# The RWKV scan of a decoder kernel: TensorE's program as two loops over rounds, one lane per direction

## The chip, the cores and the metric

The kernel runs on one core of one Trainium2 chip. The metric is the time of one execution on the device, in microseconds (us). PE is TensorE (PEld its weight loads), DVE is VectorE, ACT is ScalarE, POOL is GpSimd, SP is the engine that issues most transfers.

## The reference

The program computes a small diffusion-style decoder with 256 context tokens and 256 latent tokens: a mixer layer with two gated scans, convolutional feed-forward layers, one RWKV-7 layer, sparse attention layers, and a mixture of experts. The change concerns the recurrence of the RWKV-7 layer alone. It has 16 heads of 64 and goes over the tokens in both directions; each latent scan starts from its direction's last context state.

```python
def rwkv7_scan(r, w, k, v, kk, a, S):
    # S_t = S_{t-1} (diag(w_t) - kk_t^T (a_t * kk_t)) + v_t^T k_t ;  y_t = S_t r_t
    xs = tuple(jnp.moveaxis(t.astype(jnp.float32), 2, 0) for t in (r, w, k, v, kk, a))
    def step(S, inp):
        rt, wt, kt, vt, kkt, at = inp
        sa = jnp.einsum("bhvk,bhk->bhv", S, -kkt)
        S = S * wt[:, :, None, :] + sa[..., None] * (kkt * at)[:, :, None, :] + vt[..., None] * kt[:, :, None, :]
        return S, jnp.einsum("bhvk,bhk->bhv", S, rt)
    S, ys = lax.scan(step, S, xs)
    return jnp.moveaxis(ys, 0, 2), S
```

## The kernel before

The scan works in chunks of 64 tokens: four chunks of context, then four of latents, in each direction. A unit is a direction `d` and a group `g` of 8 heads; four units (`RW_UNITS`) are in flight, and each has eight turns (`it`), so there are 32 unit turns. Heads lie on the 128 partitions in pairs (`HALF`), four such pairs to a unit, so a tile of a unit is 128 partitions by 4 x 64 columns.

Inside a turn the token-by-token recurrence is replaced by products of 64x64 matrices. POOL scales keys and gates with exponentials of the summed decay (`beta`, `kappa`, `alpha`; DVE makes `rho`), which ACT makes (`exp`). PE then makes, by name of the step: CT (the table of removals, beta by alpha), KB (kappa and beta turned, for the state's update; in a direction's first two context and first two latent turns also V, the values turned), LK (kappa by alpha), C (alpha by beta and by the state), LKV (the masked LK by the values). The inverse of the unit triangular matrix `e` is built in five levels: Y = c by the late half columns of `e`, D = `e` turned, E = d by y, which DVE puts into `e` with a mask. ACT copies Y and D out of PSUM. Level l needs the `e` of level l-1, so Y, D, E follow each other strictly within a unit. Then U = e by w (with R, the state by rho, in the latents), O (the output, two products), and S (the state's update, two products), which DVE adds to the state and POOL scales with `last`.

The order on each engine is written out by `rwkv_steps` and `rwkv_order`: the two directions of a group stand beside each other at each step, and the second head group runs half a turn (`RW_LATER`) behind the first, so that one group's steps fill the other's waits. The program is fully unrolled: each of PE's instructions of the scan stands in the instruction stream once for each time it runs. Waits are on constants: `ScanSteps` has one semaphore for each engine and unit and numbers the steps.

The helpers of PE issue these: `cross` 8 products 64x64 by 64 columns over the four quadrants of the array (`cross_both` by 128 columns, `cross_late` by 32), `own` 8 products that keep each head half in its own rows and columns, `turn` 2 transposes of 128x128. In the trace an fp32 product is two matmul records, each with a weight load; a transpose is one.

The expert stage at the end of the program (L4912, through `rounds` at L395) already has PE loops: `pe.Fori(1, n)` with the turn's number in waits and addresses.

Of the kernel before, what the change touches and what calls it, by code (L numbers as in the profile page):

```python
# [26 lines left out]
P = 128  # L27
# [119 lines left out]
class Counter:  # L147
# [7 lines left out]
    def at(self, n):  # L155
        return self.base + n
# [11 lines left out]
class Core:  # L168
# [14 lines left out]
    def counter(self, name, keep=False):  # L183


        if name not in self.counters:
            s = self.spare.pop() if self.spare and not keep else Counter(self.nc, self.ctx, name if keep else f"{name}_{self.stage_no}")
            s.keep = keep
            self.counters[name] = s
        return self.counters[name]  # L190

# [2826 lines left out]
RW_UNITS = [(d, g) for g in (0, 1) for d in (0, 1)]  # L3018


def rwkv_kinds(it):

    return it >= RW_TURNS, it % RW_TURNS < RW_TURNS // 2


def rwkv_steps(engine):

    steps, end = [], 2 * RW_TURNS
    for it in range(end):
        latent, fresh = rwkv_kinds(it)
        along = lambda *names: [(it, name) for name in names]
        later = lambda *names: [(it + 1, name) for name in names if it + 1 < end]
        values, out = ["V"] if fresh else [], ["O"] if latent else []
        tables = [[name for name in ("CT", "RB") if name == "CT" or rwkv_kinds(i)[0]] for i in (it, it + 1)]
        reads = ["RK"] if latent else []
        if engine == "pe":
            steps += ([] if it else along("CT")) + along("KB", "LK", "C", "LKV")  # L3040
            for l in RW_LEVELS:
                steps += along(f"Y{l}", f"D{l - 1}", f"E{l}")
            steps += along("U", *out) + later("CT") + along("S")
        elif engine == "act":
            steps += along("KB", *values, "C", "LKV")
            for l in RW_LEVELS:
                steps += along(f"Y{l}", f"D{l - 1}", *([f"exp{l - 3}"] if l in (3, 4) and it + 1 < end else []))
            steps += along("U")
        elif engine == "dve":
            steps += [] if it else along("last", *tables[0])  # L3050
            steps += along("LK", *reads, "W")
            for l in RW_LEVELS:
                steps += along(f"E{l}")
            steps += later("last", *(["rho"] if it + 1 >= RW_TURNS else []))
            steps += along(*out) + later(*tables[1]) + along("S")
        else:
            steps += along("beta", "alpha", "ident") + ([(it - 1, "state")] if it else [])
    return steps


RW_SLOTS = ["KB", "LK", "C", "LKV", *(f"{kind}{l}" for l in RW_LEVELS for kind in "YDE"), "U", "O", "CT", "S"]
RW_LATER = len(RW_SLOTS) // 2


def rwkv_slot(engine, it, step):

    if engine == "pool":
        at, it = {"beta": "E4", "alpha": "E4", "ident": "U", "state": "S"}[step], it if step == "state" else it - 1
    elif step in ("CT", "RB", "last", "rho"):
        at, it = "U" if step in ("last", "rho") else "CT", it - 1  # L3070
    elif step[0] == "D":
        at = f"D{int(step[1]) + 1}"
    elif step[:3] == "exp":
        at = f"E{int(step[3]) + 3}"
    else:
        at = {"V": "KB", "RK": "LK", "W": "LKV"}.get(step, step)
    return it * len(RW_SLOTS) + RW_SLOTS.index(at)


def rwkv_order(engine):  # L3080

    lanes = [(rwkv_slot(engine, it, step) + g * RW_LATER, g, i, it, step) for g in (0, 1) for i, (it, step) in enumerate(rwkv_steps(engine))]
    return [(it, step, [unit for unit in RW_UNITS if unit[1] == g]) for _, g, _, it, step in sorted(lanes)]


class ScanSteps:


    def __init__(self, core):
        self.sems, self.at_step = {}, {}  # L3090
        for u, unit in enumerate(RW_UNITS):
            for e in ("pe", "act", "dve", "pool"):
                self.sems[e, unit] = core.counter(f"rw_{e}_step{u}")
                steps = [(it, "exp" if step[:3] == "exp" else step) for it, step in rwkv_steps(e) if step[:3] != "exp" or int(step[3]) == u % 2]
                steps = ([(-1, "exp")] if e == "act" else [(-1, "S")] if e == "dve" else []) + steps
                for i, which in enumerate(steps):
                    self.at_step[e, unit, which] = i + 1
                self.at_step[e, unit, "all"] = len(steps)

    def wait(self, eng, e, unit, it, step):  # L3100

        s = self.sems[e, unit]
        eng.wait_ge(s.sem, s.at(self.at_step[e, unit, (it, step)]))

    def done(self, ins, e, unit):
        ins.then_inc(self.sems[e, unit].sem, 1)

    def settle(self):
        for (e, unit), s in self.sems.items():
            s.n += self.at_step[e, unit, "all"]  # L3110


def rwkv_scan_stage(core, st, rw):
# [7 lines left out]


# [3 lines left out]
    TURNS, ALL = RW_TURNS, 2 * RW_TURNS  # L3126
    with ExitStack() as ctx, core.engines_block() as block:
# [5 lines left out]
        free += [st.const[:, keeps + i * N * C:keeps + (i + 1) * N * C] for i in range(2 * TT // (N * C))]  # L3133
        used_up = iter(free)
# [5 lines left out]
        names = ("kappa", "c", "e", "y", "d", "lk", "rk", "rb")  # L3140
        T = {(d, g): {n: tile(f"{n}_{d}{g}") for n in names} for d, g in RW_UNITS}
        wide = {(d, g): core.sb(f"grow_{d}{g}", [P, N, C + 2], ctx=ctx)[:] for d, g in RW_UNITS}
        last = {(d, g): core.sb(f"last_{d}{g}", [P, 2, N], ctx=ctx)[:] for d, g in RW_UNITS}
        for u, unit in enumerate(RW_UNITS):
            keys, sources = (st.H[:, 2 * u + i].rearrange("p (two n t) -> p two n t", two=2, n=N) for i in (0, 1))
            turned = core.sb(f"turned_{unit[0]}{unit[1]}", [P, 2, N, C], ctx=ctx)[:]
            T[unit].update(keys=keys, alpha=keys[:, 0], rho=keys[:, 1], sources=sources, beta=sources[:, 0], state=sources[:, 1],
                           turned=turned, kappa_t=turned[:, 0], beta_t=turned[:, 1])
            T[unit].update(u=T[unit]["c"], w=T[unit]["lk"], grow=wide[unit][:, :, 1:C + 1])
        sync = ScanSteps(core)  # L3150
        chain, zeroed = core.counter("vector_chain"), core.counter("rw_zeroed")
        mine = lambda g: slice(g * N, (g + 1) * N)
        psum = {unit: core.psum[u].rearrange("p (r x) -> p r x", r=2) for u, unit in enumerate(RW_UNITS)}

        def chunk(d, it):
# [4 lines left out]
        def val_t(unit, it):  # L3160

            d, g = unit
            local, whole = chunk(d, it)
            return (rw.val_t if it >= TURNS else rw.v)[:, mine(g), local]

        def slot(unit, n, rows=slice(0, P)):

            return psum[unit][rows, :, n * 2 * C:(n + 1) * 2 * C].rearrange("p r (j t) -> p r j t", j=2)

        def wide_slot(unit, n, rows=slice(0, P)):  # L3170

            return psum[unit][rows, :, n * 4 * C:(n + 1) * 4 * C].rearrange("p r (j two t) -> p r j two t", j=2, two=2)

        def cell(unit, r, area, rows=slice(0, P)):

            return psum[unit][rows, r, area * N * C:(area + 1) * N * C].rearrange("p (n t) -> p n t", n=N)

        def by_slot(x):

            return x.rearrange("p (j r) t -> p r j t", r=2)  # L3180

# [4 lines left out]
        def packed(x, level):  # L3186

            return x[:, 0:C // 2].rearrange("p (b h) -> p b h", h=1 << (level - 1))

        def packed_slot(unit, n):  # L3190

            return slot(unit, n)[:, :, :, 0:C // 2]

        D_AT = {1: (0, 1), 2: (1, 1), 3: (0, 1), 4: (1, 1), 5: (0, 1)}
        SLOT = {"V": 2, "Y": 1, "E": 0, "U": 0, "R": 2, "O": 3, "S": 1}
        TABLE, READ, SOURCE = 0, 1, 0
        CELL_V = (0, 1)

        @block.tensor
        def _(pe):  # L3200
            def cross(out, products):
# [17 lines left out]
            def cross_late(out, level, x, y):  # L3219
                for j in (0, 1):  # L3220
                    for s in (0, 1):
                        for r in (0, 1):
                            k = 2 * j + s
                            ins = nc.tensor.matmul(packed(out[HALF[s], r, j], level), x[HALF[r], k], y(HALF[r], k), start=True, stop=True)
# [1993 lines left out]
```

## Time and profile before

| what | value |
|---|---|
| runs | 3264.14, 3270.95 and 3374.4 us, median 3270.95 |
| the profiled execution's own time | 3275.88 us |
| its span, first to last instruction | 3274.1 us |
| busy share of the span | PE 93%, PEld 76%, DVE 72%, ACT 54%, POOL 18% |
| mean granted TensorE clock | 0.959 of full speed |
| instruction packets of queue q8 over the span | 178, 2.92 MB |

A row of a timeline merges neighbours of one form: start, microseconds to the end of the last, line, tiles, sizes, count, and in brackets the idle time before it and what ended it. A busy time of PE is modelled: a matmul record has its end some 0.2 us after its start, although the next one starts long before. So the pitch, from one group's start to the next one's, tells PE's rate, and the durations don't.

### The profile page before, as it was taken

The numbers are of one execution on the slowest core, as the hardware profiler recorded it, in microseconds if no ns is written. First come the engines' busy times: TensorE is split into PE (matmuls) and PEld (weight loads), VectorE is DVE, ScalarE is ACT, GpSimd is POOL, SyncE is SP. The second block draws the span as 40 slices with busy tenths as digits, with TensorE's granted clock in tenths as the row PEclk, the third lists the DMA queues.
The fourth block names the chain that finished last, engine by engine and source line by source line (L and its number), as shares of the span: only waits on it lengthen the run. The fifth ranks groups of instructions, "written<-read, shape, count | busy, mean of one in ns | idle before, by whom it ended". The sixth has DMA issues, their size and how long they took to land. (4 is left out here: it accounts for less than half of the span.)

```text
span 3274.1 us, 64217 instructions
## 1 busy us (share of the span) xinstructions
PE 3035.5 (93%) x25576; PEld 2480.9 (76%) x25576; DVE 2352.6 (72%) x3467; ACT 1769.2 (54%) x2875; POOL 573.8 (18%) x620
## 2 busy tenths in 40 slices
PE   5998889999797898879999999997999999999998
PEld 4775568878673777769987888856788888888887
DVE  5868754468847334577857777654899999999998
ACT  2524343232314554345436443764788888888887
POOL 0007124321101233138323111430000000000000
PEclk8998999999898999989989998998999999999999
DMA  6535224446211000158732887402999999999997
GB/s 227 170 104 19 103 90 149 142 150 204 97 58 26 4 5 4 36 187 275 272 107 78 295 311 292 124 27 79 334 371 367 373 367 367 370 363 374 368 359 262
DMA packets 337363, 647.53 MB, mean 198 GB/s; under 512 B 23853, under 2 KB 144281, under 8 KB 337113
## 3 DMA queue, kind: packets, MB, share of 16 engines
q1 hardware_dynamic: 316233, 568.38, 51.1%
q0 software_dynamic: 20160, 73.41, 6.2%
q8 instruction: 178, 2.92, 0.4%
q10 hardware_dynamic: 720, 2.23, 0.2%
q14 instruction: 72, 0.59, 0.1%
HBM read 641.34 MB, written 1.05 MB: 196 GB/s over the span
## 5 line engine op out<-in xcount | busy, mean ns | idle before, releaser
L5011 DVE TENSOR_TENSOR weights_lo<-raw_ring,weights_hi 128x1024 fp32r<-128x1024 f32 x336 | 400.9, 1220 | 36.8 <-ACT weights_hi L4941 29.4
L4941 ACT ACTIVATE weights_hi<-raw_ring 128x1024 fp32r<-128x1024 f32 x336 | 356.8, 1065 | 91.0 <-PE bank_pair L4877 54.7
L4877 PE MATMUL bank_pair<-weights_hi,expert_x_hi 128*128 128x512 f32 x896 | 282.4, 396 | 4.9 <-DVE weights_lo L5011 4.8
L5011 DVE TENSOR_TENSOR weights_lo<-H,weights_hi 128x1024 fp32r<-128x1024 f32 x224 | 268.7, 1221 | 24.7 <-ACT weights_hi L4941 17.4
L4877 PE MATMUL bank_pair<-weights_hi,expert_x_lo 128*128 128x512 f32 x896 | 277.7, 391 | 0.0
L4877 PE MATMUL bank_pair<-weights_lo,expert_x_hi 128*128 128x512 f32 x896 | 277.3, 391 | 0.0
L4941 ACT ACTIVATE weights_hi<-H 128x1024 fp32r<-128x1024 f32 x224 | 236.5, 1060 | 58.1 <-PE bank_pair L4877 43.2
L2707 DVE SCALAR_TENSOR_TENSOR conv<-bank_pair,vec,conv 128x189 f32<-128x189 f32 (+3 forms) x396 | 138.5, 428 | 147.1 <-ACT conv L2667 147.1
L4877 PEld LDWEIGHTS bank_pair<-weights_hi,expert_x_lo 128*128 128x128 f32 x896 | 168.9, 188 | 36.2
L4877 PEld LDWEIGHTS bank_pair<-weights_lo,expert_x_hi 128*128 128x128 f32 x896 | 168.7, 188 | 36.2
L4877 PEld LDWEIGHTS bank_pair<-weights_hi,expert_x_hi 128*128 128x128 f32 x896 | 164.1, 189 | 36.4 <-issue 5.1
L1341 PE MATMUL bank_pair<-Y_parts,const_parts 128*128 128x256 f32 (+1 forms) x592 | 145.8, 331 | 1.6 <-DVE H_parts L1386 1.6
L4889 PE MATMUL bank_pair<-weights_hi,hidden_hi 128*128 128x512 f32 x448 | 138.7, 391 | 0.0
L4889 PE MATMUL bank_pair<-weights_hi,hidden_lo 128*128 128x512 f32 x448 | 138.1, 389 | 0.0
L4889 PE MATMUL bank_pair<-weights_lo,hidden_hi 128*128 128x512 f32 x448 | 138.0, 389 | 0.0
L5011 DVE TENSOR_TENSOR weights_lo<-const,weights_hi 128x1024 fp32r<-128x1024 f32 x112 | 134.0, 1219 | 3.9 <-ACT weights_hi L4941 0.5
L4941 ACT ACTIVATE weights_hi<-const 128x1024 fp32r<-128x1024 f32 x112 | 119.4, 1066 | 32.0 <-PE bank_pair L4877 21.7
L621 DVE SCALAR_TENSOR_TENSOR mod_sums_ada<-mod_ring_ada,act,mod_sums_ada 128x1024 f32<-128x1024 f32 x84 | 116.5, 1391 | 6.2 <-DMA mod_ring_ada<-in_w_ada 6.2
L1341 PEld LDWEIGHTS bank_pair<-Y_parts,const_parts 128*128 128x128 f32 x592 | 101.9, 191 | 14.0 <-DVE const_parts L1321 2.4
L1130 PE MATMUL bank_pair<-const 128*128 128x512 f32 (+1 forms) x140 | 74.9, 647 | 32.8 <-PEq L206 32.8
L1341 PE MATMUL bank_pair<-H_parts,const_parts 128*128 128x256 f32 (+1 forms) x296 | 97.8, 330 | 0.0
L4889 PEld LDWEIGHTS bank_pair<-weights_lo,hidden_hi 128*128 128x128 f32 x448 | 84.1, 188 | 17.6
(805 smaller groups left out, 8128.5 us busy)
## 6 DMA issues: line engine op xcount, KB each, us to landing
raw_ring<-in_moe_w_gate SPq DMA_DIRECT2D x64, 1024.0 KB, 6.3
raw_ring<-in_moe_w_up SPq DMA_DIRECT2D x56, 1024.0 KB, 7.0
ring_up<-in_ffn_w_up SPq DMA_DIRECT2D x110, 512.0 KB, 4.1
H<-in_moe_w_down SPq DMA_DIRECT2D x48, 1024.0 KB, 5.2
raw_ring<-in_moe_w_down SPq DMA_DIRECT2D x48, 1024.0 KB, 5.2
mod_ring_ada<-in_w_ada POOLq DMA_DIRECT2D x84, 512.0 KB, 6.4
ring_down<-in_ffn_w_down SPq DMA_DIRECT2D x66, 512.0 KB, 5.9
H<-in_moe_w_gate SPq DMA_DIRECT2D x32, 1024.0 KB, 7.2
```

The lines of the kernel that those rows point to most:

```text
L621: ins = self.core.nc.vector.scalar_tensor_tensor(total, tile, scale, total, ALU.mult, ALU.add)
L1130: core.nc.tensor.matmul(core.bank(bank)[:, cols], st.C("ones"), st.const[:, cols], start=True, stop=True)
L1341: ins = self.core.nc.tensor.matmul(self.bank(it, o)[:, 0:T], w, y, start=s == self.begin[o] and k == 0 and a == 0, stop=s == self.end[o] a ...
L2707: ins = nc.vector.scalar_tensor_tensor(out, shifted, tap(w, 2 * it + o), out, ALU.mult, ALU.add)
L4877: ins = nc.tensor.matmul(bank, x[:, k * SEATS:(k + 1) * SEATS].bitcast(F32R), w[:, j * WIDE:(j + 1) * WIDE], start=k == 0 and i == 0, stop ...
L4889: ins = nc.tensor.matmul(DOWN[half], x, w[:, half * 512:(half + 1) * 512], start=c == 0 and i == 0, stop=c == FEC - 1 and i == 2)
L4941: nc.scalar.activation(hi[:, u % CUTS].bitcast(F32R), raw_part(u), ACT.Copy).then_inc(cut.sem, 1)
L5011: nc.vector.tensor_tensor(lo[:, u % CUTS].bitcast(F32R), raw_part(u), hi[:, u % CUTS], ALU.subtract).then_inc(parted.sem, 1)
```

## The change

PE's program becomes: round -1 (preparation), `pe.Fori` over rounds 0 to 7 (context), `pe.Fori` over rounds 8 to 14 (latents), and rounds 15 and 16 unrolled. A round is one turn of one head group, `m % 2`, in each of two lanes, the directions. So every tile has one address per lane, whatever the round. What this takes:

- Tiles hold the group of the round. States live in `store0` and `store1`; POOL copies the round's into `state`, and the values into `vn`. All V are turned by PE each round.
- Waits of PE are on the loop's register. So each step of ACT, DVE and POOL has a semaphore of its own per lane, counted by rounds (`ScanSignals`, with `LAG` for steps that belong to the round before), SP sets them to a common level at the start (`align`), and each wait in a loop is followed by a `sem_inc` on PE.
- U, O and S of a round are issued in the next one (`U'`, `S'`, `O'`); CT, C (now CC) and LK in the round before (`fore`).
- In the context D is made by products with the identity (`turn_by_product`) in place of transposes; in the latents by transposes.
- RK and RB are made together after `rho` is there (RKB); one ACT copy takes the turned kappa, beta and values (768 columns), one takes U and R; one DVE copy takes both halves of CC. DVE copies `e1`, the identity with level 1, into `e` in each round. POOL adds R to the output, DVE adds O.
- `rho` moves from DVE to POOL.

```diff
-RW_UNITS = [(d, g) for g in (0, 1) for d in (0, 1)]
+RW_ROUNDS = 4 * RW_TURNS
+RW_READS = 2 * RW_TURNS
+LANES = (0, 1)
...
+def rwkv_order(engine, n):
+    late, read, more = n >= 1, n >= RW_READS, n + 1 < RW_ROUNDS
+    inside = 0 <= n < RW_ROUNDS
...
+    fore = [lane(d, "CT+", "CC+", "LK+") if more else [] for d in LANES]
+    reads, behind, kept = ["RKB"] * read, ["O'"] if n > RW_READS else [], ["S'"] if more else []
+    if engine == "pe":
+        if n < 0:
+            return fore[0] + fore[1]
+        if read:
+            behind = ["O'"]
+        if not inside:
+            return both("U'", *behind)
+        return [*both("Y2", "D1", *["R"] * read, "U'"), *both("E2", *kept, *behind), *both("Y3", "D2"), *both("V", "KB"), *both("E3", "LKV"), *both("Y4", "D3", *reads), *both("E4"),
+                *both("Y5", "D4"), *both("E5"), *lane(0, "Y6", "D5"), *fore[0], *lane(1, "Y6", "D5"), *fore[1], *both("E6")]
+    if engine == "act":
+        scales = both("shrink+", "grow+") if more else []
...
+        return [*both("Y2", "D1", *behind), *scales, *both("Y3", "D2"), *both("KB"), *both("Y4", "D3"), *both("Y5", "D4"), *both("Y6", "D5")]
+    if engine == "dve":
...
+        return [*both("copy"), *both("E2", *kept, *behind), *both("E3", "LKV"), *both(*reads), *both("E4"), *both("E5"), *fore[0], *fore[1], *both("E6"), *last]
...
+    ahead = [*both("ident+"), *both("alpha+"), *(both("scale'") if late and more else []), *both("state+", "vn+"), *both("beta+", "kappa+")] if more else []
+    return [*ahead, *(both("rho+") if more and n + 1 >= RW_READS else []), *both(*["R"] * (read and inside))]
...
+            def turn_by_product(out, x):
+                return cross(out, [(x, ident)])
+
+            def rounds_from(n, at):
+                def wait(e, lane, step):
+                    pe.wait_ge(sig.sems[e, lane, step].sem, at)
+                    if not isinstance(at, int):
+                        pe.sem_inc(carried.sem, 1)
+                        carried.n += times
...
+                    elif kind == "Y":
+                        if l == 2:
+                            wait("dve", d, "E6")
+                            wait("dve", d, "CC")
+                        else:
+                            wait("dve", d, f"E{l - 1}")
+                        e = t["e1" if l == 2 else "e"]
+                        ins = cross_late(Y[d], l, lambda rows, k: t["c"][rows, k], lambda rows, k: half_columns(e[rows, k], l, 1 - d))
+                    elif kind == "D":
+                        ins = (turn if n >= RW_READS else turn_by_product)(TURN[d], t["e1" if l == 1 else "e"])
...
+            for first, end in ((0, RW_READS), (RW_READS, RW_ROUNDS - 1)):
+                times = end - first
+                with pe.Fori(at(first), at(end)) as i:
+                    rounds_from(first, i)
+            rounds_from(RW_ROUNDS - 1, at(RW_ROUNDS - 1))
+            rounds_from(RW_ROUNDS, at(RW_ROUNDS))
```

## Rows read from the trace of the kernel before

**Rows 1.** A line's own view: durations min/median/max in ns, first to last start.
```profile
L3435 DVE TENSOR_TENSOR H<-H,bank_pair x32: 420/421/423, 1092.9 to 1372.0; 128x256 f32<-128x256 f32 x32
```

**Rows 2.** Windows: the scan, and five turns of the expert loop.
```profile
1058.00:1373.00 315.00, 282.62 (x10049) 245.93 (x10050) 126.78 (x398) 158.15 (x520) 93.06 (x152) 0.98 0.02 4
...
2600.00:3198.00 598.00, 597.89 (x2741) 495.61 (x2740) 560.38 (x519) 485.00 (x506) 0.00 (x0) 1.00 1.01 367
```

**Rows 3.** Timeline of PE in the context part of the scan.
```profile
1090.59 0.67 PE L3224 MATMUL bank_pair<-y,d 64*64 64x32 f32 x32 [0.16 <-ACT d L3351]
1091.08 0.67 PE L3207 MATMUL bank_pair<-H 64*64 64x64 f32 x32
1091.57 0.62 PE L3224 MATMUL bank_pair<-e,c 64*64 64x32 f32 x32
...
1150.10 1.10 PE L3216 MATMUL bank_pair<-H 64*64 64x128 f32 x32
1151.14 0.66 PE L3236 MATMUL bank_pair<-const 128*128 128x128 f32 x4
1151.72 0.33 PE L3230 MATMUL bank_pair<-rw_v,lk 64*64 64x64 f32 x4
...
1154.98 0.65 PE L3224 MATMUL bank_pair<-const 64*64 64x32 f32 x32
1155.57 0.66 PE L3236 MATMUL bank_pair<-const,e 128*128 128x128 f32 x4
...
1158.83 0.67 PE L3230 MATMUL bank_pair<-const 64*64 64x64 f32 x16
1159.32 0.53 PE L3230 MATMUL bank_pair<-lk,const 64*64 64x64 f32 x12
1160.42 0.33 PE L3230 MATMUL bank_pair<-lk,const 64*64 64x64 f32 x4 [0.57 <-issue]
```

**Rows 4.** Timeline of PE in the latent part.
```profile
1259.42 0.38 PE L3236 MATMUL bank_pair<-const,kappa 128*128 128x128 f32 x2
...
1259.95 0.66 PE L3265 MATMUL bank_pair<-const,rw_v 128*64 128x128 f32 x8
1260.54 0.33 PE L3236 MATMUL bank_pair<-const,kappa 128*128 128x128 f32 x1
```

**Rows 5.** Waits in the scan: us in total, times, longest.
```profile
PEld bank_pair L3236 <- issue: 7.2, 27, 1.1
```

**Rows 6.** DMA queues, in the scan and from 2600 us on: packets, MB, share.
```profile
q8 instruction: 79, 1.29, 1.7%
...
q14 instruction: 2, 0.02, 0.0%
```

**Rows 7.** Lines' own views: the expert loop's branches, the scan's separate waits.
```profile
L399 PEldq COMPARE_BRANCH  x7: 76/208/238, 2539.6 to 3257.4; - x7
...
L3103 PEldq EVENT_SEMAPHORE  x56: 51/51/51, 1090.9 to 1345.1; - x56
```

**Rows 8.** Groups of instructions in the scan: busy us, mean ns, idle before.
```profile
L3416 DVE COPY_PREDICATED e<-const,bank_pair 128x128 f32<-128x128 uint32 x80 | 22.6, 332 | 48.0 <-PE bank_pair L3224 47.8
L3344 ACT ACTIVATE y<-bank_pair 128x128 f32<-128x128 f32 x80 | 21.1, 278 | 34.4 <-PE bank_pair L3224 34.4
L3340 ACT ACTIVATE turned<-bank_pair 128x512 f32<-128x512 f32 x32 | 18.3, 596 | 17.5 <-PE bank_pair L3265 16.2 <-PE bank_pair L3236 1.3
L3369 POOL TENSOR_TENSOR kappa<-rw_k,kappa 128x256 f32<-128x256 f32 x16 | 11.7, 730 | 1.3
L3426 DVE TENSOR_TENSOR lk<-bank_pair,const 128x256 f32<-128x256 f32 x24 | 9.8, 422 | 2.7 <-PE bank_pair L3216 1.3 <-PE bank_pair L3207 0.9
...
L3421 DVE COPY_PREDICATED e<-const,bank_pair 128x256 f32<-128x256 uint32 x16 | 7.0, 463 | 0.6 <-PE bank_pair L3207 0.4
L3353 ACT ACTIVATE c<-bank_pair 128x256 f32<-128x256 f32 x16 | 6.2, 384 | 7.7 <-PE bank_pair L3230 7.4
L3404 DVE COPY last<-grow 128x4 f32<-128x4 f32 x30 | 3.4, 159 | 0.0
```

More of the change, by code:

```diff
@@ L3017 @@
 RW_TURNS = CTX // RW_CHUNK
-RW_UNITS = [(d, g) for g in (0, 1) for d in (0, 1)]
[L3021 to L3058, printed above, removed]
@@ L3061 @@
[L3061 to L3077, printed above, removed]
@@ L3080, in rwkv_order @@
[L3080 to L3086, printed above, removed]
-    def __init__(self, core):
[L3090 to L3106, printed above, removed]
+RW_ROUNDS = 4 * RW_TURNS
@@ new lines, with value, first, align @@
+class ScanSignals:
+    LAG = {"U": 1, "S": 1, "O": 1, "E6": 1, "kappa": -1}
+    STEPS = {"act": ("D1", "D2", "D3", "D4", "D5", "U", "KB", "grow", "shrink"),
+             "dve": ("CC", "LK", "E2", "E3", "E4", "E5", "E6", "S", "O", "LKV", "RKB", "last", "copy"),
+             "pool": ("alpha", "kappa", "rho", "scale", "R")}
+    def __init__(self, core):
+        self.sems = {(e, lane, s): core.counter(f"rw_{e}_{s}_{lane}") for e, steps in self.STEPS.items() for lane in LANES for s in steps}
+        self.level = max(c.base for c in self.sems.values()) + 1
+        self.pe = [core.counter(f"rw_pe_steps_{lane}") for lane in LANES]
+        self.pe_at, self.pe_n = {}, 0
+        for n in range(-1, RW_ROUNDS + 1):
+            for d, step, m in rwkv_order("pe", n):
+                if d == 0:
+                    self.pe_n += 1
+                    self.pe_at[step, m] = self.pe_n
+    def value(self, step, m):
+        return self.level + m + 1 + self.LAG.get(step, 0)
+    def first(self, step):
+        return RW_READS if step in ("R", "RKB", "rho", "O") else -1 if step in ("U", "S") else 0
+    def align(self, eng):
+        for (e, lane, s), c in self.sems.items():
+            by = self.value(s, self.first(s) - 1) - c.base
+            if by:
+                eng.sem_inc(c.sem, by)
+    def wait_pe(self, eng, lane, step, m):
+        eng.wait_ge(self.pe[lane].sem, self.pe[lane].at(self.pe_at[step, m]))
+    def wait(self, eng, e, lane, step, m):
+        eng.wait_ge(self.sems[e, lane, step].sem, self.value(step, m))
+    def done(self, ins, e, lane, step, m):
+        if (e, lane, step) not in self.sems:
+            return
+        c = self.sems[e, lane, step]
+        ins.then_inc(c.sem, 1)
+        c.n = self.value(step, m) - c.base
@@ L3108, in settle @@
     def settle(self):
-        for (e, unit), s in self.sems.items():
-            s.n += self.at_step[e, unit, "all"]
+        for c in self.pe:
+            c.n += self.pe_n
 def rwkv_scan_stage(core, st, rw):
@@ L3139, in tile @@
             return t.rearrange("p (n t) -> p n t", n=N)
[L3140 to L3155, printed above, removed]
+        names = ("shrink", "kappa", "alpha", "rho", "e1", "e", "y", "d", "lk", "w", "vn", "store0", "store1")
+        T = [{n: tile(f"{n}_{d}") for n in names} for d in LANES]
+        wide = [core.sb(f"grow_{d}", [P, N, C + 2], ctx=ctx)[:] for d in LANES]
@@ L3157, in chunk, with mine @@
+        sig = ScanSignals(core)
+        cleared, zeroed, emptied, stores, carried = (core.counter("rw_" + n) for n in ("cleared", "zeroed", "emptied", "stores", "pe_waited"))
+        front, levels = ([core.psum[2 * d + i].rearrange("p (r x) -> p r x", r=2) for d in LANES] for i in (0, 1))
+        def mine(m):
+            return slice(m % 2 * N, (m % 2 + 1) * N)
+        def chunk(d, m):
+            it = m // 2
             c = it % TURNS if d == 0 else TURNS - 1 - it % TURNS
             return slice(c * C, (c + 1) * C), slice((it >= TURNS) * CTX + c * C, (it >= TURNS) * CTX + (c + 1) * C)
[L3160 to L3176, printed above, removed]
+        def slot(pair, n):
+            return pair[:, :, n * 2 * C:(n + 1) * 2 * C].rearrange("p r (j t) -> p r j t", j=2)
@@ L3384, in _ @@
         @block.vector
         def _(dve):
-            c = Chain(dve, chain)
-            for unit in RW_UNITS:
+            for d in LANES:
                 for edge in (0, C + 1):
-                    ins = nc.vector.memset(wide[unit][:, :, edge:edge + 1], 1.0)
+                    ins = nc.vector.memset(wide[d][:, :, edge:edge + 1], 1.0)
             zeroed.count(ins)
-            for unit in RW_UNITS:
-                sync.done(nc.vector.memset(T[unit]["state"], 0.0), "dve", unit)
-            c.ended(nc.vector.memset(rw.y, 0.0))
@@ L3394, in _ @@
-            for it, step, units in rwkv_order("dve"):
-                for unit in units:
-                    d, g = unit
-                    t = T[unit]
-                    kind = step.rstrip("123456")
+            for d in LANES:
+                for name in ("e", "w", "ur", "turned"):
+                    ins = nc.vector.memset(T[d][name], 0.0)
+            cleared.count(ins)
+            for d in LANES:
+                nc.vector.memset(T[d]["rkb"], 0.0)
+            emptied.count(nc.vector.memset(rw.y, 0.0))
@@ L3436, in _ @@
-                    sync.done(ins, "dve", unit)
-        sync.settle()
+                        ins = nc.vector.tensor_copy(last[d][:, m % 2].unsqueeze(2), t["grow"][:, :, edge:edge + 1])
+                        sig.done(ins, "dve", d, step, m)
+                        continue
+                    if step == "copy":
+                        sig.wait_pe(dve, d, "U", m - 1)
+                        sig.wait(dve, "dve", d, "CC", m)
+                    elif step == "S":
+                        sig.wait_pe(dve, d, "O" if m + 1 >= RW_READS else "S", m)
+                    else:
+                        sig.wait_pe(dve, d, {"CT": "LK", "CC": "LK"}.get(step, step), m)
```

410 lines of the change are left out of this document (238 added, 172 removed).

## The prediction

> **What bounds the kernel now.** The page's busy slices and the windows view come first. TensorE (PE) is the busiest engine of the whole span, but the diff touches one stage alone, the RWKV scan. It starts on PE at 1058 us (the edge of the window in [rows 2]), and DVE's last addition to a state ends at 1372.4 [rows 1]: 314 us, 9.6% of the 3274.1 us span. In that stretch PE is busy 282.6 us (90%), ACT 50%, DVE 40%, POOL 30%, and DMA moves 4 GB/s [rows 2]. So nothing but the scan's order of work can move the time, and PE is the nearest bound.
>
> Next comes what PE's time consists of. The timeline of PE gives the pitch of a block, start to start, where nothing waits. I call a block the 16 matmul records that one helper makes for one unit (8 matmuls, each in two passes; a transpose is one record).
> - Y or E, 32 columns: two blocks in 1091.08-1090.59 = 0.49 us, 0.245 each. CT by `cross`, 64 columns: 1091.57-1091.08, the same 0.245; the columns don't count here [rows 3].
> - `cross_both`, 128 columns: 1.04 for two, 0.52 each. `own`: 1159.32-1158.83 = 0.49 each [rows 3].
> - Four transposes: 1259.95-1259.42 = 0.53 with nothing switched, so 0.26 a pair; 1151.72-1151.14 = 0.58 with the way back to 64x64. Y before a transpose takes 1155.57-1154.98 = 0.59 instead of 0.49. Going from 64x64 to 128x128 and back costs about 0.1 us each way [rows 3, 4].
> - The V turn by eight products with the identity: 0.59 [rows 4].
>
> **Work of PE before.** A unit's turn in the context: CT 0.25, KB 0.53, V 0.3 (half the turns), LK 0.25, C 0.52, LKV 0.49, ten Y/E 2.45, five D 1.55 with the switches shared by two units, U 0.49, S 0.49 = 7.3 us. In the latents CT and LK are wide (+0.54), R and O come on (+0.98): 8.8. Sixteen of each: 258 us of 314. The other 56 us are stalls; PE's busy time hides a part of them, since a record's modelled end reaches 0.2 us past the next one's start.
>
> What these waits are, by the view of waits: but for the first wait of the stage the largest kind of idle PE and of idle weight loads is "issue", a wait for nothing that the profile shows [rows 5]. The timeline shows it inside blocks that are underway: 0.57 us at 1160.42, twelve records into an `own` block that had begun at 1159.32 [rows 3]. Data can't be missing there. The instruction queue q8 brought 79 packets and 1.29 MB in the stretch, 16 KB per packet, against 20,099 matmuls and loads [rows 2, 6]: 64 bytes each, 256 a packet, one each 4.0 us. I take the stalls to fall on the borders of the fetched pieces. The loads' waits by issue are 0.27 us on the mean before transposes (7.2/27) [rows 5]; 79 x 0.28 = 22 us, with 0 and 79 x 0.57 = 45 us as the ends. The rest, some 34 us, is waits for ACT and DVE.
>
> **The change, part by part.** Lanes: before, four units are in flight; after, two (one per direction), each alternating its head groups over 16 rounds. The same 32 unit turns are done.
>
> (1) PE work after. A context round per lane: Y/E 2.45; D as eight products, 5 x 0.245 = 1.23, without a switch; U and S 0.98; V and KB three pairs of transposes, 0.83 with their switches; LKV 0.49; CT, CC, LK 1.02 = 7.0. Latents: D stays a transpose but is now one lane's at a time (`both("Y3", "D2")` is lane by lane), so 0.26 + 0.16 = 0.42 x 5 = 2.1; R, O and RKB add 1.47 = 9.3. Two lanes: 14.0 and 18.7 us a round, 8 of each: 261 us. Against 258 it is +3 us. The new D saves 0.3 per turn in the context and loses 0.55 in the latents. PE's work as such brings nothing.
>
> (2) Fetching. Two loop bodies, about 1,470 and 1,510 instructions (716 and 736 matmul records, as many loads, 34 and 40 waits), the unrolled rounds -1, 15 and 16 about 1,900: 19 pieces instead of 79. 60 borders x 0.28 = -17 us, if a body stays in place. For that speaks the expert loop: 598 us of it hold 5,481 matmuls and loads in five turns [rows 2], about 1,100 a turn, and in the 670 us from 2600 on q8 has no packet, only q14 two small ones [rows 6]. The new bodies are a third larger than that one. The Trainium skill, "Runtime: NRT & Kernel Launch", section "Instruction fetch mechanics", says both: PE holds 2,048 instructions, and a taken branch whose target is outside the current window forces a fetch before execution goes on. By its capacity the bodies stay; by its branch rule they don't, which is rival B. The trace of the expert loop agrees with the first, at the smaller size.
>
> (3) Turning back. A turn of PE's loop in the trace costs an ALU_OP, a FUSED_REGOPS of some 0.04 and a COMPARE_BRANCH of 0.208 [rows 7], about 0.3 us; there it was hidden by queued 0.39 us matmuls, here nothing is queued. 8 + 7 turns: +4 us (bounds 1 and 15, the last if the first block waits 1 us for its instructions).
>
> (4) The waits. Each wait in the loops is a register's and is followed by a `sem_inc`. The trace has 56 EVENT_SEMAPHORE on PE at 51 ns in the scan [rows 7]; 37 a round x 16 x 0.051 = 30 us if all were on the path, 0 if all are hidden. Most are satisfied early and overlap queued matmuls; 6 or 7 a round really wait. +6 us.
>
> (5) What the shorter cover costs. This is the largest term, stepped from the durations in [rows 8] (ACT 0.28 for Y and for a D of the same size, DVE E 0.33 and a little more, 0.42 for 256 columns and 0.16 for 4, so 0.68 for 512; ACT 0.38 for 256, 0.60 for 512, so 0.81 for 768), plus 0.25 from a PE block's last start to a reader's start. Context round, Y2 of lane 0 at 0: PE has Y2, D1, U' of both lanes done by 2.0, E2 and S' by 3.5, Y3 and D2 by 4.5, V and KB by 6.0, E3 and LKV by 7.8, all with ACT and DVE in time but for 0.3 us. Levels 4 and 5 have no filler: Y and D of both lanes 1.0, then E waits for ACT, the next Y for DVE's E: Y4 to Y6 of lane 0 takes 5.0 (4.8 by ACT's denser pitch) where PE has 3.5 of work. The end of the round is worse. DVE does CT, CC, LK of both lanes before E6: 2 x (0.46 + 0.68 + 0.42) = 3.1 us, at best 2.7, starting when PE has LK of lane 0. PE has issued E6 of lane 1 some 1.75 us after that start, DVE ends E6 of lane 0 2.7 + 0.36 = 3.1 us after it, and the next round's Y2 waits for that: 1.4 us of idle PE each round. Sum 17.1 us against 14.0 of work. Latents, the same way: RKB fills level 4 on PE but puts 1.4 us ahead of E4 on DVE (0.9 stall), level 5 stalls 0.4, the end 1.4: 21.4 against 18.7. POOL has kappa' ready about 1.6 us before CT needs it and is no wait yet (14 operations of up to 0.73, 8.4 to 10 us of a context round).
>
> The sum: first Y2 at about 1062.4 (PE waits for POOL, which now has stores, identities, alpha, state and value copies ahead of beta and kappa, and for DVE's `CT`, `CC`, `LK`), 8 x 17.1 + 8 x 21.4 = 308, less 3.4 in round 15, which prepares nothing, plus 3.5 for the closing U and O: 1370.5, that is 2 us earlier than now [rows 1]. On it come waits +6, turns back +4, and the 19 cold borders, 19 x 0.28 = +5. **Scan +13 us.** The profiled execution took 3275.9 us (span 3274.1), 5 us over the median of the runs. 3275.9 + 13 = 3289, as a median 3284.
>
> **The rivals.**
> - A: the filler works better than stepped. Then PE's work is what counts: 261 + 4 at the start + 10 for waits, turns and cold borders + 10 to 20 of waits, 285 to 295 against 314: -25 us, 3246. For it: ACT and DVE are at 50% and 40% now. Against: E6 stands behind both lanes' CT, CC, LK in DVE's own order, which no slack elsewhere removes. Its floor, 261 + 4, is -49 us: 2% (65 us) is out of reach while PE does this work.
> - B: the body doesn't stay in place and each turn fetches again. Then the 5 to 6 borders return, 15 x 5.5 x 0.28 = 23 us, and each jump waits for its first piece (a packet takes 1.7% x 16 x 315 / 79 = 1.1 us [rows 6]), 15 to 20 us: 3284 + 40 = 3324. Decides from the body's size somewhere above 1,100 instructions.
> - C: slower by over 2%. Two lanes are too few: each of the five levels is Y, D on PE (0.49) + 0.25 + ACT 0.50 + 0.05 + E 0.25 + 0.25 + DVE 0.36 + 0.05 = 2.2 us, and what stands between on the in-order engines delays the chain; if POOL's kappa' comes 2 us late too (POOL's operations 0.1 longer beside DVE, and started only when `grow` is through ACT's queue behind U'), a round takes 21 and 25.5, the scan 376: +62, 3333 and up. It decides when a round's chain is over 20 us; by my steps it is 17 to 21.
> - D: the loops change nothing, the fetch stalls being something else. Then -17 in (2) falls away and the rest stays: 3301.
>
> **How the numbers follow.** Forecast within its own terms (3265 to 3305) 0.42; A 0.24; D 0.10; B 0.16; C 0.08. Range 3236 to 3326: below are the best parts of A, above C and the worst of B. A measurement of this kernel tells 2% from no change. Faster by over 2% asks for more than PE's floor allows, 0.03; slower by over 2% is C and a corner of B, 0.09; within 0.88.
>
> **What the profile after would show.** Rounds of 17 and 21 us; PE work of 14 and 18.7 in them. Instruction packets in the scan: about 19, none after each loop's first turn. Idle PE by "issue" under 15 us. The largest wait of PE: Y2 for DVE's E6, about 1.4 us in each of 15 rounds. EVENT_SEMAPHORE on PE about 600 times. The other stages unchanged within a few us. I am wrong if PE's waits per round are under 1 us (A), if packets keep coming at 4 GB/s (B), or if CT waits for POOL (C).

## The result, and the profile after

| | median, us | lowest to highest | runs |
|---|---|---|---|
| before | 3271.75 | 3264.14 to 3374.4 | 18 |
| after | 3287.8 | 3277.26 to 3292.22 | 18 |

The run of 3374.4 us is a slow one, 3% above the others, and the ratio leaves it out. The ratio is 1.0045, with a 95% interval of 1.0034 to 1.0055; the medians differ by 16 us, after being the slower. The forecast was 3284. The profiled execution has a span of 3285.9 us, 11.8 more than before. The scan, from the end of DVE's drain ahead of it to DVE's last operation in it, goes from 1055.9 to 1394.9 in the trace of after and from 1052.6 to 1372.4 in that of before: 339.0 against 319.9, 19.1 us longer. All the rest together is 7.3 us shorter (3.4 longer ahead of the scan, 10.7 shorter behind it); over the traces of this study the rest varies by 14 us (2940.3 to 2954.2), though all edits of the experiments lie in the scan. So the scan alone is explained below.

The page of after: busy time, share of the span and instructions, and the instruction queue over the span. Before had 178 such packets.

```profile
PE 3040.2 (93%) x27176; PEld 2492.1 (76%) x27176; DVE 2371.4 (72%) x3483; ACT 1743.1 (53%) x2797; POOL 615.4 (19%) x720
...
q8 instruction: 117, 1.92, 0.2%
```

The queues of the scan alone, 1050 to 1400 us of after (79 packets before [rows 6]):

```profile
q8 instruction: 18, 0.29, 0.4%
```

The lines of the loops and of the separate semaphore counts, durations min/median/max in ns, first and last start:

```profile
L3350 PEldq COMPARE_BRANCH  x15: 76/208/235, 1086.3 to 1371.4; - x15
...
L3280 PEldq EVENT_SEMAPHORE  x552: 51/51/51, 1065.1 to 1371.0; - x184
```

The branches mark the turns. The windows view, cut at them: length, busy us (and instructions) of PE, its loads, DVE, ACT and POOL, granted clock, DMA share and GB/s. In order: the first context turn, the fifth, the first latent turn, and two steady latent turns.

```profile
1064.90:1086.20 21.30, 16.78 (x728) 15.28 (x725) 8.68 (x25) 8.03 (x28) 6.13 (x12) 0.98 0.01 4
...
1137.40:1154.50 17.10, 14.96 (x732) 14.05 (x727) 8.15 (x24) 8.05 (x28) 7.20 (x14) 1.00 0.00 0
1205.70:1235.30 29.60, 24.30 (x750) 21.06 (x744) 9.39 (x27) 8.71 (x28) 9.94 (x18) 0.79 0.01 3
1280.10:1301.80 21.70, 19.19 (x751) 16.81 (x746) 10.04 (x28) 8.67 (x28) 9.89 (x18) 1.00 0.00 1
1301.80:1326.40 24.60, 22.10 (x750) 19.31 (x743) 10.05 (x28) 8.71 (x28) 9.90 (x18) 0.86 0.00 0
```

Context turns 2 to 8 take 17.0 to 17.2 us, all at a granted clock of 1.00. The latent turns 2 to 7 take 23.1, 21.7, 21.7, 24.6, 21.7 and 23.1; the longer ones are those with a clock under 1.00. The first turn of each loop is the one that fetches, 5 packets in the context and 6 in the latents; the fourth context turn has one more, the others none.

PE's waits by what ended them, in the scan: us in total, times, longest.

```profile
PE bank_pair L3258 <- DVE const L3489: 27.6, 23, 1.5
PE bank_pair L3241 <- POOL const L3419: 10.9, 1, 10.9
PE bank_pair L3241 <- issue: 4.7, 4, 1.5
PE bank_pair L3258 <- ACT const L3391: 3.2, 16, 0.2
PE bank_pair L3258 <- issue: 2.3, 3, 1.6
```

L3258 is `cross_late` (Y and E), L3489 DVE's E. PE's timeline has these waits in each steady turn (start, length, idle time before it): Y2 in a context turn, then in a latent turn Y2, Y5 and the second lane's E5, which waits for ACT's copy of D4.

```profile
1139.33 0.43 PE L3258 MATMUL bank_pair<-const,cw 64*64 64x32 f32 x16 [1.49 <-DVE const L3489]
...
1282.02 0.43 PE L3258 MATMUL bank_pair<-const,cw 64*64 64x32 f32 x16 [1.50 <-DVE const L3489]
1295.82 0.43 PE L3258 MATMUL bank_pair<-const,cw 64*64 64x32 f32 x16 [0.74 <-DVE const L3489]
1297.99 0.43 PE L3258 MATMUL bank_pair<-Y,H 64*64 64x32 f32 x16 [0.26 <-ACT H L3391]
```

The first wait stands at the head of each of 15 rounds, 1.5 us in most and never under 1.1, 21.8 of the 27.6 us; Y5 in the eight latent rounds gives the rest. The wait by "issue" is 7.0 us in 7 pieces. In before the same view has four such rows:

```profile
PE bank_pair L3207 <- issue: 4.4, 6, 1.3
PE bank_pair L3230 <- issue: 3.4, 7, 0.7
PE bank_pair L3236 <- issue: 2.3, 4, 1.0
PE bank_pair L3224 <- issue: 2.2, 6, 0.8
```

That is 12.3 us in 23 pieces. Against before, then, 61 fewer packets took only 5 us out of PE's own idle time. Its waits for DVE, added over all rows of the view, went the other way: from 9.6 to 27.9 us. With those for ACT and POOL the idle time is 14.7 us longer, most of the scan's 19.1.

### The profile page after: what moved, and what is told of

Its sections match the earlier page's. It is cut to its first block and busy times, and to the rows that moved or that the text cites. A ratio compares the mean times of both kernels' runs of the same rounds, so it can differ in the third digit from the quotient of the medians.

```text
span 3285.9 us, 68297 instructions
## 1 busy us (share of the span) xinstructions
PE 3040.2 (93%) x27176; PEld 2492.1 (76%) x27176; DVE 2371.4 (72%) x3483; ACT 1743.1 (53%) x2797; POOL 615.4 (19%) x720
## 5 line engine op out<-in xcount | busy, mean ns | idle before, releaser
L3384 ACT ACTIVATE const<-bank_pair 128x128 f32<-128x128 f32 x80 | 22.5, 282 | 150.3 <-PE bank_pair L3269 80.7
```

The costliest lines, as they stand in the source:

```text
L3384: nc.scalar.activation(by_slot(t["y"])[:, :, :, 0:C // 2], Y[d], ACT.Copy)
```

## Experiments

Each ratio is to before on the same chip. The changed kernel itself, run again with the first group (`e0_after`): 3285.14 us, 1.0056 (1.0041 to 1.0071), steady turns of 17.1 and 21.7 us, scan 1.2 us shorter than in the first trace. Its latent turns at a lower clock stand elsewhere (23.2 and 23.1, at turns 3 and 5), so as far as two traces tell their places are chance. One falls in the context here, in its second turn:

```profile
1085.30:1103.90 18.60, 16.57 (x736) 15.65 (x731) 8.13 (x25) 8.24 (x28) 7.20 (x14) 0.91 0.00 0
```

> The changed kernel as it is, as the yardstick on this chip. Both theories: about 1.0045 of the kernel before, 3280 to 3292 us; context rounds 17.1 us, latent rounds 21.7 us where the clock is full. If the half-clock stretches inside the scan (five of 3.4 us and one of 10.2 us in the first profile) are a matter of chance, their places will differ here; if the stalls at fixed places bring them, they will be at the same rounds.

**The same order without loops.** PE's loops are written out: no register in a wait, no `sem_inc`.

```diff
-            for first, end in ((0, RW_READS), (RW_READS, RW_ROUNDS - 1)):
-                times = end - first
-                with pe.Fori(at(first), at(end)) as i:
-                    rounds_from(first, i)
+            for n in range(RW_ROUNDS - 1):
+                rounds_from(n, at(n))
```

> PE's rounds 0 to 14 stand in the stream one after the other, with constant waits and no sem_inc; all else as in the changed kernel. Theory S (small borders, the prediction's: 0.28 us each): about 60 pieces come back, +17 us, the separate waits (-6) and the turns back (-4) go: +7 us against the changed kernel. Rival F (a border costs what the cold first context round shows, 21.3 - 17.1 = 4.2 us for 6 pieces, 0.7 each): 7 x 4.2 in the context and as much or more in the latents, +60 us and more less 10: +50 us. Rival N (the fetch stalls are nothing): -10 us. q8 packets in the scan 80 in all cases.

3308.8 us, 1.0138 (1.0122 to 1.0154). The instruction queue has 91 packets in the scan (80 were expected). A context turn takes 19.8 to 21.4 us instead of 17.1, with 5 or 6 packets each; PE's waits by "issue":

```profile
PE bank_pair L3258 <- issue: 14.8, 15, 1.9
PE bank_pair L3241 <- issue: 14.8, 18, 1.2
...
PE bank_pair L3269 <- issue: 1.3, 1, 1.3
PE bank_pair L3250 <- issue: 1.2, 1, 1.2
```

32.1 us in 35 pieces, 25 more than with the loops; the medians differ by 24, where the three theories had 7, 50 and -10. The gain of the loops lies mostly in the context: from one KB copy of ACT to the next, latent rounds at full clock take 21.5 to 23.0 us unrolled, on the mean only 0.6 over the 21.7 with the loop. So the loops do work, and the loss is elsewhere: the new order unrolled is 42 us over before, and the loops give 24 of it back. But what they remove is in part of the new order's own making: before had 12.3 us of such idle time with 79 packets, the new order unrolled has 32.1 with 91.

**Without loops, but with the separate counts.** As above, and each wait of rounds 0 to 14 keeps its `sem_inc`.

```diff
-                    if not isinstance(at, int):
+                    if 0 <= n < RW_ROUNDS - 1:
                         pe.sem_inc(carried.sem, 1)
```

> As the unrolled one, but each wait of rounds 0 to 14 is followed by a sem_inc on PE, as in the loops. The difference to the unrolled one is the price of the separate waits alone. Theory S: +6 us (0.05 us at the 6 or 7 waits of a round that really wait). Rival H (hidden): within 2 us. Rival G (each of the 550 costs its 51 ns): +28 us.

3381.62 us, 1.0339 (1.0319 to 1.0358): 1.0339 / 1.0138 is 2%, so 552 counts add 66 us to the unrolled kernel, 0.12 us each, with two more packets. All three theories (6, under 2, 28) were too low. Rounds take 22.4 to 31.3 us. This isn't the price of a count by itself: PE's idle time by "issue" doubles, from 32.1 to 64.1 us in 54 pieces (its two largest rows first), and the clock falls far more often:

```profile
PE bank_pair L3241 <- issue: 33.5, 26, 2.3
...
PE bank_pair L3258 <- issue: 22.9, 21, 2.2
```

```profile
1058.00:1485.00 427.00, 330.72 (x11532) 294.89 (x11528) 144.08 (x410) 134.30 (x446) 130.08 (x240) 0.86 0.02 4
```

**Twice the counts in the loops.**

```diff
-                        pe.sem_inc(carried.sem, 1)
-                        carried.n += times
+                        for _ in (0, 1):
+                            pe.sem_inc(carried.sem, 1)
+                            carried.n += times
```

> The changed kernel with two sem_inc behind each wait in the loops in place of one. The unrolled pair differed by 66 to 80 us for one sem_inc at each of 550 waits. Theory X (in the loops, where nothing is fetched, a sem_inc hides unless the wait really waits): 51 ns at 7 waits, +0.3 us a round at most, +0 to +6 us. Rival G (a sem_inc costs 0.12 us anywhere): 37 x 0.12 = 4.4 us a round, +66 us; then the loops lose as much as they gain.

3327.81 us, 1.0188 (1.0175 to 1.0202), by the ratios 1.3% or 43 us over the changed kernel, between the 0 to 6 and the 66 of the two theories. The scan has 18 packets, as before the edit, so this is no fetching. A context turn at full clock:

```profile
1190.90:1209.90 19.00, 15.77 (x735) 14.61 (x729) 8.31 (x25) 8.05 (x28) 7.22 (x14) 1.00 0.00 0
```

1.9 us for 34 more counts, 0.056 each. A latent round without lowered clock, from one KB copy of ACT to the next, takes 22.8 against 21.7: 1.1 for 40. On top, most turns have a stretch at the lower clock (20.4 and 24.3). So in the context 0.056 us of each count comes through, no less than the 0.051 that it lasts, and in the latents about half of it: most counts are on the path, and not only those where PE really waits.

**E6 ahead of the second lane's CT, CC, LK.** The part that changes of the order on PE, then of that on DVE:

```diff
- *both("E5"), *lane(0, "Y6", "D5"), *fore[0], *lane(1, "Y6", "D5"), *fore[1], *both("E6")]
+ *both("E5"), *both("Y6", "D5"), *fore[0], *both("E6"), *fore[1]]
...
- *both("E5"), *fore[0], *fore[1], *both("E6"), *last]
+ *both("E5"), *fore[0], *both("E6"), *fore[1], *last]
```

> PE and DVE do E6 of both lanes before CT, CC, LK of lane 1 (lane 0's stay ahead of E6). Theory Q (the 1.5 us at Y2 is DVE's queue in front of E6): Y2 finds E6 done; the wait moves to lane 1's CC, which comes 1 us of PE work later; a round gets 1.0 to 1.5 us shorter, -15 to -22 us. Rival P (the chain of POOL or ACT is next behind it): the 1.5 us appear at another wait and the time stays within 3 us.

3265.31 us, 1.0000 (0.9985 to 1.0015), 20 us under the changed kernel. Y2's wait, and the windows of a context and a latent turn:

```profile
1134.68 0.43 PE L3258 MATMUL bank_pair<-const,cw 64*64 64x32 f32 x16 [0.51 <-DVE const L3489]
```

```profile
1133.60:1149.80 16.20, 15.03 (x725) 14.09 (x720) 7.96 (x25) 8.04 (x28) 7.21 (x14) 1.00 0.00 0
1287.10:1307.90 20.80, 19.29 (x746) 16.88 (x741) 9.95 (x29) 8.67 (x28) 9.91 (x18) 1.00 0.00 0
```

0.9 us of each of 15 rounds, 14 us; no steady latent turn has a lowered clock any more, which gives most of the rest.

**And E4 ahead of RKB on DVE.** On top of the last edit, the part that changes on DVE:

```diff
- *both(*reads), *both("E4"), *both("E5")
+ *both("E4"), *both(*reads), *both("E5")
```

> E6 ahead of lane 1's CT, CC, LK, and besides DVE does E4 of both lanes before RKB of both. Theory Q (0.74 us at Y5 is DVE's RKB in front of E4): it goes, latent rounds 20.8 -> 20.1 us, 8 rounds, -6 us against the run with E6 ahead alone, 0.998 of the kernel before. Rival: the wait moves to CT of lane 0, which needs RKB: no change.

3263.88 us, 0.9993 (0.9979 to 1.0008). Latent turns of 20.4; the wait at Y5:

```profile
1299.78 0.43 PE L3258 MATMUL bank_pair<-const,cw 64*64 64x32 f32 x16 [0.36 <-DVE const L3489]
```

0.74 became 0.36, 0.4 us a turn as in its length (0.7 was expected). This is the best kernel here with the whole computation, and not measurably different from before.

**D by transposes everywhere.**

```diff
-  ins = (turn if n >= RW_READS else turn_by_product)(TURN[d], t["e1" if l == 1 else "e"])
+  ins = turn(TURN[d], t["e1" if l == 1 else "e"])
...
```

E on PE and the copy on ACT follow with the layout of `d`.

> D is made by transposes of 128x128 in the context too. Theory W (work of PE counts): +0.175 us for each of ten D blocks of a round, of which those of levels 4 and 5 partly fall in waits for ACT, 8 rounds: +8 to +14 us against the changed kernel. Rival: if the two lanes are bound by the chain through ACT and DVE, under +4 us. If wide transposes next to 64x64 products bring the half-clock stretches, these appear in the context as well.

3305.71 us, 1.0093 (1.0076 to 1.011). That is 0.4% or 12 us over the changed kernel by the ratios. Context turns of 18.5 at full clock (the second takes 17.5), 20.0 with a lowered stretch:

```profile
1105.30:1123.80 18.50, 16.48 (x592) 14.09 (x588) 8.17 (x25) 8.27 (x28) 7.20 (x14) 1.00 0.00 0
1123.80:1143.80 20.00, 17.98 (x594) 15.41 (x587) 8.34 (x25) 8.26 (x28) 7.21 (x14) 0.91 0.00 0
```

The products save 1.4 us a context turn, 0.14 per D, although a turn has 140 more matmul records with them.

**D by products everywhere.** The same lines with `turn_by_product` and its layout alone.

> D is made by eight products with the identity in the latents too, not by transposes of 128x128. Theory W (work of PE counts): each D block 0.42 with its switches becomes 0.245, 10 a round, -1.75 us a round if all of it is on the path, -1.0 where E4 and E5 wait for ACT anyway: 8 rounds, -8 to -14 us. The latent body grows from about 1,510 to about 1,790 instructions. Rival B (it no longer stays in place): packets of q8 in every latent round, six or seven each, and +4 us or more a round, +20 to +40 us.

3321.89 us, 1.018 (1.0162 to 1.0198). The latent body grows from 1,515 instructions of PE to 1,795 (five levels of 56). Two latent turns of this kernel, cut at the branches, the packets of the first, the branch's line, and PE's wait behind the first turn's branch:

```profile
1289.90:1324.00 34.10, 24.14 (x885) 22.72 (x884) 10.08 (x28) 8.68 (x28) 9.98 (x18) 0.80 0.02 5
1324.10:1343.90 19.80, 17.76 (x896) 16.97 (x891) 10.00 (x29) 8.57 (x28) 9.91 (x18) 0.99 0.00 0
```

```profile
q8 instruction: 9, 0.15, 1.9%
```

```profile
L3350 PEldq COMPARE_BRANCH  x15: 76/213/4847, 1085.8 to 1413.8; - x15
```

```profile
1294.52 0.65 PE L3258 MATMUL bank_pair<-const,cw 64*64 64x32 f32 x16 [3.93 <-issue]
```

Of the five turns from 1255 on four take 34 to 35 us, with 9 packets each, and begin with a branch of 4.1 to 4.8 us behind which PE stands idle by "issue". The one between, with a branch of 0.223, has no packet and takes 19.8, 1.9 less than with transposes. The products are the better D here too; what they cost is the body's place.

**Both edits.** E6 ahead, and products everywhere.

> E6 ahead of lane 1's CT, CC, LK and D by products everywhere. If both gains are real and independent: -23 to -36 us against the changed kernel, that is 8 to 22 us faster than the kernel before. If they share one wait: no better than the better of the two.

3308.14 us, 1.0109 (1.0087 to 1.0131). Context turns of 16.2, latent ones again fetching: three of 34.4 to 35.9 us, and between them 18.5 to 19.9. From products alone to this the ratio falls by 0.0071, and E6 alone gave 0.0056: within the intervals the two edits add up.

**Products in two, and in four, of the five latent levels,** on top of both moves on DVE. In these two kernels half of `d` stands in the other layout in the levels that changed, so part of E is computed from other elements; the instructions, sizes and order are those named.

> As the last, and D4 and D5 of the latents by products: body of about 1,624 instructions against 1,512. If it stays in place: D4 and D5 0.175 shorter in both lanes, -0.7 us a round, less where E5 waits for ACT, -2 to -6 us, 0.997 of the kernel before. If it doesn't: packets in each latent round and +4 to +7 us a round.

> As the last with D2 to D5 by products: about 1,736 instructions. The body of 1,792 was fetched again. If the border is the 2,048 of a page, less what lies unused at both ends, either may hold. If it stays: -5 to -11 us against E4 ahead alone, some 0.995 of the kernel before. If not: packets, and +30 to +50 us.

Two levels, 1,627 instructions: 3261.26 us, 0.9981 (0.997 to 0.9991), latent turns of 19.8, no packet of q8 in the last five of them:

```profile
1264.30:1284.10 19.80, 18.58 (x801) 16.82 (x796) 9.83 (x29) 8.65 (x28) 9.91 (x18) 1.00 0.00 1
```

Four levels, 1,739 instructions: 3304.02 us, 1.0105 (1.0084 to 1.0127), and 27 packets over the last five latent turns:

```profile
q8 instruction: 27, 0.44, 1.5%
```

```profile
L3350 PEldq COMPARE_BRANCH  x15: 76/212/4932, 1087.0 to 1387.4; - x15
```

The turns alternate, 34.0, 19.1, 33.7, 18.6, 34.1 us; the second and third:

```profile
1281.90:1301.00 19.10, 18.63 (x861) 17.48 (x857) 9.56 (x28) 8.66 (x28) 9.96 (x18) 0.96 0.00 1
1301.00:1334.70 33.70, 22.42 (x852) 20.28 (x847) 10.57 (x31) 8.70 (x28) 9.92 (x18) 0.85 0.02 5
```

So a body of 1,627 instructions stays in place here, and one of 1,739 doesn't. Where the body begins in the stream was not varied by itself.

**Two rounds per turn in the context,** 2,936 instructions of PE.

```diff
+            with pe.Fori(at(0), at(RW_READS), 2) as i:
+                rounds_from(0, i)
+                rounds_from(1, i + 1)
...
```

> The context loop turns four times over two rounds each: its body is about 2,930 instructions, twice the changed kernel's. If a body stays in place only up to some 2,000 instructions: every turn fetches again, 11 to 12 packets a turn, and each context round costs what the cold one does, 21 us in place of 17: +25 to +30 us. If any body stays: no packets after the first turn and the same time but for the register's addition at each wait (34 x 0.03 us in every second round, +4 us at most).

3358.45 us, 1.0268 (1.0246 to 1.0289). That is 2.1% or some 69 us over the changed kernel by the ratios, where 25 to 30 were expected. Each turn of two rounds fetches, 13 packets and 51 to 54 us for what takes 34 in the changed kernel:

```profile
L3349 PEldq COMPARE_BRANCH  x4: 79/3367/3548, 1107.8 to 1264.7; - x4
```

The three taken branches last 3.3 to 3.5 us instead of 0.2.

## Why the prediction was right, and what in it was not

The size was right (+19 in the scan for +13), and the mechanism named as the largest was too. That the size came so near is partly luck: several terms were wrong by more than their sum shows, in opposite directions.

- **The queue on DVE, step (5): right.** 1.4 us at Y2 in each of 15 rounds was forecast, 1.5 measured, and moving E6 made the round 0.9 shorter. Latent waits at Y5 and E5 were 0.74 and 0.26 for the 0.9 and 0.4 of the text. Rounds of 17.1 and 21.7 stand against 17.1 and 21.4.
- **But the stepped round should have been longer than measured.** 17.1 was stepped without waits' counts and turning back, and 17.1 is what these kernels take with them. The doubling says that 34 counts cost 1.9 us. If the first 34 cost the same, the steps were 2 us a round too long, and the error of step (4) fell on the same place with the other sign. From Y2 to Y4 to Y6 to the next Y2 of lane 0 the trace has 7.33, 4.80 and 4.95 us (starts at 1139.33, 1146.66, 1151.46 and 1156.41) for 7.8, 5.0 and 4.3 stepped. So the first two parts were short of the steps even with their counts in. How the counts divide over the parts isn't shown.
- **Step (4), the separate counts: mis-sized.** +6 was taken. 552 at 0.056 in the context and 0.028 in the latents would be 15 + 8 = 23 us, inside the 0 to 30 of the text, and that at full clock. The reason given, that most waits are satisfied early and so hidden, is what failed: a second count behind each wait cost 0.056 us in the context, although PE idles at few of these waits.
- **Step (3), turning back: +4 was taken, and little of it was due.** The branch lasts 0.21 us as forecast. But in the steady turn shown above it is through at 1280.4, and PE then stands idle until Y2 at 1282.02, when DVE's E6 is there: the turn back lies inside the wait that step (5) had already counted. No run prices it alone.
- **Step (2), the fetching: mechanism right, price wrong.** 18 packets for 19 forecast, none in the steady turns. But I multiplied the 60 borders that go by a mean of PE's loads before transposes, 0.28, for 17 us; PE's own idle time by "issue" was 12.3 us over 79 packets, 0.16 each, and fell by 5. What the loops are worth against the same order unrolled is another matter: 24 us with the counts in the loops and none outside. In the new order a border costs more, 32.1 / 91 = 0.35 us of idle PE, and a context turn with 5 or 6 of them is 2.7 to 4.3 us longer than in the loop, although it has no counts.
- **What the forecast gave to the loops and to the order:** loops -17 +4 +6 +5 = -2, the rest +15. Measured: loops -24 (3285.14 - 3308.8), the rest +42 (3308.8 - 3267.21). Both were too small, in opposite directions, and that the sum came out is luck. Moving E6 gave 20 and E4 some 3, both tried with the loops in place. The 19 that are left are as much as the unrolled order has more of idle PE by "issue" than before (32.1 against 12.3); that the one is the other wasn't tested.
- **The cold turns and the clock: undersized.** +5 for 19 cold borders. The first context turn is 4.2 over a steady one, the first latent turn 7.9, with two waits by "issue" (1.4 and 1.6 us) and a clock of 0.79 over the turn. Where the clock stayed at 1.00 in it, in the kernel with two levels by products, it was 5.2 us over a steady one (25.0 for 19.8), so being the first turn, with its fetching, is the larger part, and the clock the smaller. Steady latent turns lose another 5.8 us in all to four stretches of lowered clock, which the text didn't have.
- **D, step (1): about right.** By its figures a D of one lane is 0.42 by transposes and 0.245 by a product, 1.75 us for the ten of a round. Transposes cost 1.4 us in each of 8 context rounds, 11 us, and with the lowered clock 17 in the scan; in the latents they are the dearer D as well, 1.9 us a turn where the body is in place. The 0.3 per turn of the text is against before's transposes, whose switches two units share, and no run tests that.
- **Rivals.** A: PE's waits for DVE rose to 27.9 us from 9.6, so the filler did not cover; taking 14 to 16 us out of the rounds by moving E6 and E4 gives 0 to -2 us against before, not -25. B: at 1,515 instructions no; the same mechanism at 1,739 and up, with branches of 3.3 to 4.9 us and 9 to 13 packets, where I had 15 to 20 us in all for 15 jumps. In these kernels it decides between 1,627 and 1,739; the text had only "somewhere above 1,100". The Trainium skill, "Runtime: NRT & Kernel Launch", section "Instruction fetch mechanics", gives PE 2,048 instructions, and lets a taken branch out of the window wait for its page. The traces agree with the wait (3.93 us idle at one such branch), and with pieces of 256 instructions (0.29 MB in 18 packets); not with the capacity as a loop can use it, since 1,739 didn't stay. C: POOL is busy 7.2 of 17.1 us and PE waits for it only once, at the start, 10.9 us (10.2 before). D: the unrolled kernel excludes it, by 24 us.

What stays open: what makes the some 20 us that E6 and E4 don't explain, and why a border costs more PE time in the new order (two lanes in place of four is one difference, one address per tile another); why a body of 1,739 is fetched in every second turn and not in each; and what the loops would give if the products themselves carried the wait on the register, without counts. That was not tried.

## What to carry to other kernels

Count a loop body's instructions on PE before giving it a loop: up to 1,627 a taken branch lasted 0.2 us here, at 1,739 up to 4.9 us and the body came again. When a rewrite brings an order and a mechanism at once, price them apart, by unrolling the new order: here the mechanism was worth 24 us and the order cost 42, and part of the 24 may be dearer fetching that the order had brought. Look on each engine for what stands ahead of the operation that the next round begins with; here one exchange of lists, on PE and DVE, gave back all of the loss.

## What was not expected of the hardware

- A separate count on PE lasts 51 ns in the trace and costs 0.03 to 0.06 us of a dense stream that is in place, 0.12 in one that is being fetched, where the longer stalls by "issue" and the lower clock are part of it.
- A loop body a little too large is fetched in one turn (9 packets) and not at all in the next (34.0 and 19.1 us at 1,739 instructions; at 1,795 one of five turns was without), so one turn looked at alone misleads.
- TensorE's granted clock fell to 0.50 (1.2 GHz) for 3.4 us at a time inside steady turns, mostly latent ones. In the changed kernel one such stretch began at 1304.6, 0.8 us after the 1.50 us wait at Y2, three others 0, 0.2 and 0.5 us after the pair of waits of 0.74 and 0.26 at Y5 and E5. With Y2's wait at 0.51 none was left in the steady turns. That the waits bring the stretches isn't shown: the third, fourth and sixth latent turns have the same waits and none of them. A turn with one takes 1.4 us more. The windows of one and of the 3.4 us behind it, and PE's timeline at its start:

```profile
1304.60:1308.00 3.40, 3.40 (x64) 3.00 (x64) 0.30 (x1) 1.67 (x5) 0.40 (x1) 0.50 0.00 0
1308.00:1311.40 3.40, 3.40 (x202) 3.36 (x200) 2.06 (x6) 1.82 (x5) 1.73 (x4) 1.00 0.01 2
```

```profile
1304.46 1.06 PE L3264 MATMUL bank_pair<-const,H 64*64 64x64 f32 x16
1305.30 0.95 PE L3264 MATMUL bank_pair<-const 64*64 64x64 f32 x13
```

An `own` block has a pitch of 1305.30-1304.46 = 0.84 us here, for the 0.49 of [rows 3].
